# Down-projection of two MLP slices as seven block products: a Strassen-like scheme carried from the up-projection into the down-projection

## The reference

```
def _squared_relu_mlp(h, w1, w2):
    return jnp.square(jax.nn.relu(h @ w1)) @ w2
...
x = x + _squared_relu_mlp(_rmsnorm(x, norm_mlp[i]), mlp_w1[i], mlp_w2[i])
```

## Time and profile before

| what | value |
|---|---|
| median of 3 runs | 2006.91 us |
| the profiled execution | 2007.59 us, span 2005.8 us |
| busy: PE, PEld, DVE, ACT, POOL | 1993.7, 1743.6, 1376.8, 1062.6, 304.9 us |
| granted TensorE clock | 1.000 |
| HBM read | 223.05 MB |

### The profile page before, as it was taken

How to read it: one execution, slowest core, us unless ns; L and a number is a source line. 1 busy time by engine, 2 the same in 40 slices (tenths; PEclk the granted TensorE clock), 3 DMA queues, 4 the chain that set the end, 5 groups by cost and what they waited for, 6 DMA issues and landing times.

```text
span 2005.8 us, 28783 instructions
## 1 busy us (share of the span) xinstructions
PE 1993.7 (99%) x11760; PEld 1743.6 (87%) x11760; DVE 1376.8 (69%) x1634; ACT 1062.6 (53%) x1508; POOL 304.9 (15%) x371
## 2 busy tenths in 40 slices
PE   9999999999999999999999999999999999999998
PEld 7888898989878889899888889898988888899897
DVE  6866865655898777556698786564687758656564
ACT  6655643625467646254456663453547646354363
POOL 7102000000200200002731200000741011000000
PEclk9999999999999999999999999999999999999999
DMA  6212455545222264474332145544532123474651
GB/s 189 68 59 66 142 128 159 146 95 158 89 90 84 86 166 141 102 190 102 117 90 71 54 150 143 156 132 112 163 83 72 55 72 122 110 193 102 160 145 42
DMA packets 190610, 230.94 MB, mean 115 GB/s; under 512 B 18864, under 2 KB 133104, under 8 KB 190480
## 3 DMA queue, kind: packets, MB, share of 16 engines
q1 hardware_dynamic: 158192, 198.62, 31.7%
q0 software_dynamic: 29888, 29.11, 9.2%
q10 hardware_dynamic: 2400, 1.38, 0.2%
HBM read 223.05 MB, written 2.10 MB: 112 GB/s over the span
## 4 chain that ended last, share of the span: by engine, by line
PE 95%; DVE 2%; POOL 1%; ACT 0%; issue 0%; DMA 0%; DVEq 0%; ACTq 0%; POOLq 0%
PE psum L708 29%; PE psum L710 29%; PE psum L709 29%; PE psum L1151 2%; PE psum L1124 1%; PE psum L1259 1%; DVE h_lo L1544 1%; PE psum L1100 1%; PE psum L1096 1%; PE psum L1095 1%; PE psum L1101 1%; PE psum L1094 0%; PE psum L1361 0%; PE psum L1391 0%; PE psum L1377 0%
## 5 line engine op out<-in xcount | busy, mean ns | idle before, releaser
L1517 DVE TENSOR_TENSOR w_lo<-w_raw,w_hi 128x1024 fp32r<-128x1024 f32 (+1 forms) x307 | 378.4, 1237 | 255.7 <-ACT w_hi L2456 254.3
L2456 ACT ACTIVATE w_hi<-w_raw 128x1024 fp32r<-128x1024 f32 (+1 forms) x311 | 328.5, 1061 | 386.1 <-PE psum L710 362.5
L708 PE MATMUL psum<-u_hi,w_hi 128*128 128x512 f32 x1256 | 492.4, 392 | 1.2 <-issue 1.2
L710 PE MATMUL psum<-u_hi,w_lo 128*128 128x512 f32 x1256 | 489.2, 389 | 0.0
L709 PE MATMUL psum<-u_lo,w_hi 128*128 128x512 f32 x1256 | 489.1, 389 | 0.0
L708 PE MATMUL psum<-h_hi,w_hi 128*128 128x256 f32 (+1 forms) x1368 | 440.6, 322 | 1.7 <-DVE w_lo L1517 1.3
L709 PE MATMUL psum<-h_lo,w_hi 128*128 128x256 f32 (+1 forms) x1368 | 437.4, 320 | 0.0
L710 PE MATMUL psum<-h_hi,w_lo 128*128 128x256 f32 (+1 forms) x1368 | 437.3, 320 | 0.0
L708 PEld LDWEIGHTS psum<-u_hi,w_hi 128*128 128x128 f32 x1256 | 235.9, 188 | 50.9 <-issue 1.9
L708 PEld LDWEIGHTS psum<-h_hi,w_hi 128*128 128x128 f32 x1368 | 260.2, 190 | 22.2 <-DVE w_lo L1517 1.8
L710 PEld LDWEIGHTS psum<-u_hi,w_lo 128*128 128x128 f32 x1256 | 235.8, 188 | 49.6
(11 more groups left out here) (342 smaller groups left out, 2662.9 us busy)
## 6 DMA issues: line engine op xcount, KB each, us to landing
w_raw<-in_mlp_w SPq DMA_DIRECT2D x192, 512.0 KB, 3.9
arena<-in_mlp_w SPq DMA_DIRECT2D x88, 512.0 KB, 4.7
w_raw<-in_mlp_w POOLq DMA_DIRECT2D x36, 512.0 KB, 7.2
w_raw<-in_mla_w_o SPq DMA_DIRECT2D x16, 512.0 KB, 3.7
w_raw<-in_lru_w_in SPq DMA_DIRECT2D x16, 512.0 KB, 3.8
arena<-in_mlp_w POOLq DMA_DIRECT2D x12, 512.0 KB, 6.6
w_raw<-in_swa_w_in SPq DMA_DIRECT2D x12, 512.0 KB, 3.9
w_raw<-in_mla_w_ukv SPq DMA_DIRECT2D x8, 512.0 KB, 4.7
```

What stands on the lines that cost most here:

```text
L708: nc.tensor.matmul(out, stat[0], mov[0], start=start, stop=False, skip_group_check=skip)
L710: return nc.tensor.matmul(out, stat[1], mov[0], start=False, stop=stop, skip_group_check=skip)
L1517: ins = nc.vector.tensor_tensor(w_lo[:, to], tile, exact(w_hi[:, to]), ALU.subtract)
L2456: nc.scalar.activation(w_hi[:, to], raw_tile(op.raw), ACT.Copy).then_inc(w_hi_done, 1)
```

## The change

In slices 1 and 2 of every MLP (`TURNED_DOWN`), the eight units of the down-projection become two rounds (g = 0, 1) of seven products, 14 units of 24 matmuls over 256 columns. For this the relu output is first multiplied by the norm factor and then squared (so the down result can be added to x as it is), and four sums of its blocks are formed on VectorE ("turned"), all seven operands being split. Results are added to x straight out of PSUM in nine steps per round, in place of `add_scaled`. Up rounds of these slices are `scaled_round`. Not shown: `group` is moved out of `seven_products` unchanged, cos and sin share a tile, `w2_block` names 512 x 256 blocks of w2, and the raw buffer of the sum p is declared free two products earlier.

```diff
+    def blocks_of(block):
+
+        a, e, b = (Raw(block(half, n), phase, True) for half, n in ((0, 0), (1, HALF), (1, 0)))
+        p = Raw(block(0, 0), phase, True, plus=block(0, HALF))
+        q = Raw(block(0, HALF), phase, True, plus=block(1, HALF))
+        return a, e, b, p, q
+
...
-        q.freed = len(ops)
+        p.freed = q.freed = len(ops)
...
-        p.freed = b.freed = len(ops)
...
+    def seven_down(i, s, g):
+
+        nonlocal sums
+
+        def block(half, n):
+            return ("w2_block", i, s * SLICE + half * T, g * T + n, BLOCK)
+
+        a, e, b, p, q = blocks_of(block)
+        raws.extend((a, q, b, p, e))
+        ops.append(Operand("A11", a))
+        a.freed = len(ops)
+        ops.append(Operand("A21+A22", q))
+        q.freed = len(ops)
+        ops.append(Operand("A12", b))
+        ops.append(Operand("A11+A21", p, (p, e)))
+        ops.append(Operand("A11+A21+A22", p, (b, p), made=sums + 1))
+        ops.append(Operand("A22", e))
+        p.freed = e.freed = len(ops)
+        ops.append(Operand("A11+A12+A21+A22", b, made=sums + 2))
+        b.freed = len(ops)
         sums += 2
 
...
             for g in range(2):
+                if s in TURNED_DOWN:
+                    seven_down(i, s, g)
+                    continue
...
+TURNED_DOWN = (1, 2)
...
+        minus_t1, t1_raw = tile(u_lo_f32, 1), tile(u_lo_f32, 0)
+        U11 = tile(u_hi, 0), tile(arena_r, relu_at), kept[0][0]
+        UT1 = tile(u_hi, 1), tile(u_lo, 0), t1_raw
+        U21 = tile(u_hi, 2), tile(u_lo, 2), kept[1][0]
+        UT3 = tile(u_hi, 3), tile(arena_r, relu_at + 1), kept[0][1]
+        UT2 = tile(u_lo, 3), tile(u_lo, 1), minus_t1
+        UT4 = sq_r[:, :], tile(arena_r, tables_at), kept[1][0]
+        U22 = trig_r[:, :], tile(arena_r, tables_at + 1), kept[1][1]
...
+            def seven_down(g):
+
+                xy, own = (0, 1) if g == 0 else (2, 3)
+                d = c.now("downs")
+                c.add("downs")
+                n = 7 * (d // 2)
+                x1, y, z, v = bank(xy, 0), bank(xy, 1), bank(own, 0), bank(own, 1)
+                claim(xy)
+                pe.wait_ge(u_turned, n + 1)
+                group(x1, U11, False)
+                claim(own)
+                pe.wait_ge(u_turned, n + 2)
+                group(v, UT1, False)
+                pe.wait_ge(u_turned, n + 3)
+                group(y, U21, False)
+                pe.wait_ge(u_turned, n + 4)
+                group(z, UT3, False)
+                pe.wait_ge(u_turned, n + 5)
+                pe.wait_ge(x_added, 7 * d + 1)
+                group(x1, UT2, True)
+                pe.wait_ge(u_turned, n + 6)
+                pe.wait_ge(x_added, 7 * d + 5)
+                group(z, UT4, True)
+                pe.wait_ge(u_turned, n + 7)
+                pe.wait_ge(x_added, 7 * d + 7)
+                group(x1, U22, True)
...
+                    if s in TURNED_DOWN:
+                        seven_down(0)
+                        seven_down(1)
+                    elif last and s + 1 == SLICES:
...
+            def u_low(n, k, operand):
+
+                high, low, raw = operand
+                dve.wait_ge(u_high, 7 * n + k)
+                nc.vector.tensor_tensor(low, raw, exact(high), ALU.subtract).then_inc(u_turned, 1)
+
+            def by_rstd(to, source, j):
+
+                k = to.shape[1] // HALF
+                rows = rstd[:, j * HALF:(j + 1) * HALF].unsqueeze(1).to_broadcast([P, k, HALF])
+                return nc.vector.scalar_tensor_tensor(out=by_chunk(to), in0=by_chunk(source), scalar=0.0, in1=rows,
+                                                      op0=ALU.max, op1=ALU.mult)
+
+            def scaled_round(g, n):
+
+                xy, own = (0, 1) if g == 0 else (2, 3)
+                first, other = kept[g]
+                d11, d21, d12, d22 = first[:, 0:T], first[:, T:2 * T], other[:, 0:T], other[:, T:2 * T]
+                r = c.now("rounds")
+                c.add("rounds")
+                c.add("tensor_unit", 3)
+                split(1)
+                if g == 1:
+                    dve.wait_ge(u_squared, 4 * n + 2)
+                    nc.vector.tensor_tensor(t1_raw, *kept[0], ALU.subtract).then_inc(u_turns, 1)
+                split(1)
+                if g == 1:
+                    u_low(n, 1, U11)
+                split(1)
+                product_passed()
+                dve.wait_ge(c_copied, 3 * r + 1)
+                nc.vector.tensor_tensor(d11, bank(xy, 1), d11, ALU.add).then_inc(c_added, 1)
+                split(1)
+                product_passed()
+                dve.wait_ge(c_copied, 3 * r + 3)
+                nc.vector.tensor_tensor(d22, d22, bank(xy, 0), ALU.subtract).then_inc(c_added, 1)
+                if g == 1:
+                    u_low(n, 2, UT1)
+                split(1)
+                product_passed()
+                free(nc.vector.tensor_tensor(d21, bank(own, 0), d21, ALU.subtract), own)
+                dve.wait_ge(c_added, 2 * r + 2)
+                by_rstd(d22, d22, 1)
+                dve.wait_ge(area_free[own], c.now(f"area{own}"))
+                by_rstd(first, first, 0).then_inc(scaled, 1)
+                split(1)
+                product_passed()
+                free(by_rstd(d12, bank(xy, 0), 1), xy)
+                split(1)
...
+            def seven_down(g, n):
+
+                xy, own = (0, 1) if g == 0 else (2, 3)
+                d = c.now("downs")
+                c.add("downs")
+                x1, y, z, v = (by_chunk(bank(xy, 0)), by_chunk(bank(xy, 1)), by_chunk(bank(own, 0)),
+                               by_chunk(bank(own, 1)))
+                x11, x12, x21, x22 = (x_block(g, i, j) for i in range(2) for j in range(2))
+
+                def add(to, sums, after, op=ALU.add):
+                    dve.wait_ge(x_added, 7 * d + after)
+                    return nc.vector.tensor_tensor(to, to, sums, op)
+
+                if g == 0:
+                    u_low(n, 3, U21)
+                    dve.wait_ge(u_squared, 4 * n + 4)
+                    nc.vector.tensor_tensor(kept[0][1], kept[0][1], kept[1][1], ALU.subtract).then_inc(u_turns, 1)
+                    dve.wait_ge(u_high, 7 * n + 2)
+                    nc.vector.tensor_tensor(minus_t1, minus_t1, kept[1][1], ALU.subtract).then_inc(u_turns, 1)
+                product_passed()
+                add(x11, x1, 0).then_inc(x_added, 1)
+                split(1)
+                if g == 0:
+                    u_low(n, 4, UT3)
+                    dve.wait_ge(u_turns, 4 * n + 3)
+                    nc.vector.tensor_tensor(kept[1][0], kept[1][0], minus_t1, ALU.add).then_inc(u_turns, 1)
+                    u_low(n, 5, UT2)
+                product_passed()
+                add(x22, v, 0, ALU.subtract).then_inc(x_added, 1)
+                add(x12, v, 0).then_inc(x_added, 1)
+                split(1)
+                product_passed()
+                add(x11, y, 1).then_inc(x_added, 1)
+                if g == 0:
+                    u_low(n, 6, UT4)
+                product_passed()
+                add(x22, z, 2).then_inc(x_added, 1)
+                split(1)
+                if g == 0:
+                    u_low(n, 7, U22)
+                split(1)
+                product_passed()
+                add(x21, x1, 0, ALU.subtract).then_inc(x_added, 1)
+                add(x22, x1, 5, ALU.subtract).then_inc(x_added, 1)
+                split(1)
+                product_passed()
+                free(add(x21, z, 6), own)
+                split(1)
+                product_passed()
+                free(add(x12, x1, 3), xy)
+                split(1)
+                for a in (own, xy):
+                    dve.wait_ge(area_free[a], c.now(f"area{a}"))
...
+                    if s in TURNED_DOWN:
+                        n = c.now("downs") // 2
+                        for g in range(2):
+                            scaled_round(g, n)
+                        for g in range(2):
+                            seven_down(g, n)
+                        continue
...
+            def u_high_of(operand):
+
+                high, low, raw = operand
+                nc.scalar.activation(high, raw, ACT.Copy).then_inc(u_high, 1)
+
+            def square_in_place(t):
+                nc.scalar.activation(t, t, ACT.Square).then_inc(u_squared, 1)
+
+            def scaled_round(g, n):
+
+                xy, own = (0, 1) if g == 0 else (2, 3)
+                first, other = kept[g]
+                d11, d21, d12, d22 = first[:, 0:T], first[:, T:2 * T], other[:, 0:T], other[:, T:2 * T]
+                r = c.now("rounds")
+                c.add("rounds")
+                product_passed()
+                if g == 0:
+                    act.wait_ge(u_ready, c.now("u_ready"))
+                nc.scalar.activation(d11, bank(xy, 0), ACT.Copy).then_inc(c_copied, 1)
+                split(1)
+                if g == 1:
+                    u_high_of(U11)
+                split(1)
+                if g == 1:
```

(51 more changed lines are left out.)

55 lines of the change are left out of this document (36 added, 19 removed).

## The result

| | before | after |
|---|---|---|
| median of 4 runs | 2006.89 us (2006.59 to 2007.75) | 2110.53 us (2109.27 to 2112.02) |
| the profiled execution | 2007.59 us, span 2005.8 | 2112.02 us, span 2110.2 |
| HBM read | 223.05 MB | 248.21 MB |

The changed kernel takes 1.0516 times as long (95% interval 1.0498 to 1.0534): 103.6 us more, where 102 were forecast.

The account below looks back on a forecast made before the run. TensorE, busy 99% of the span, was taken as the bound. 28 products of 2.86 us plus six stalls gave 96.3 us a slice against 83.54, 102 us more over 8 slices: 2110 us, range 2062 to 2132.

Parts of the forecast that it names:

- What TensorE gains: Changed slice: 14 products replace 8 units, 40.04 us instead of 43.52, a gain of 3.48 us, 27.8 in all.
- What the helpers get: Changed slice: VectorE's 72.7 us fit TensorE's 80.1, but 24.8 against 20.0 us in g = 0, so order decides.
- The costs without a row before: New scaling steps on VectorE: taken at the times of plain sums; the upper bound used 0.75 us for 512 columns.
- The walk: Hand walk through a changed slice's handovers: TensorE stalls of 1.3, 1.0, 6.0, 5.0, 1.2 and 1.7 us.
- P18: 18th product, down-projection g = 0: TensorE stalls 5.0 us, waiting for VectorE's low part of UT3.
- The clock rival: TensorE's clock falls in the stalls, a product takes at least 5.1 us: 0 to 2 us a slice, 2110 to 2126; chance 0.25.
- The period: Time between like rows of changed slices: near 96 us, 96.3 by the sum, against 83.54 before.
- the tightest load: Sum p of g = 1: load lands about 78, split due at 76.7, product at 85; costs nothing, might cost 1 us.
- "No stall" in g = 1: Second down round: VectorE has 15.7 us of work in 20 us and catches up, so TensorE has no stall.
- "Too dark": Rival: stalls before the 17th and 18th products are half as long, a slice takes 90.8 us, time 2065; chance 0.13.
- "hidden": Rival: a slice's stalls together fall under 3.48 us, TensorE stays the bound; 1980 with none; chance 0.05.

Follow-up runs that it names:

- `e_both_light`: Changed kernel with steps reordered and ScalarE's copies earlier, both sums of weights of g = 0 left out, three sums of squares cut to 8 columns: 2000.26 us.
- experiment 5: Changed kernel with the same steps of ScalarE and VectorE in another order, all work kept, copies not moved: 2039.87 us.
- experiment 7: Changed kernel with one VectorE sum of weights per changed slice left out: 2099.39 us where left out in g = 0, 2107.94 us in g = 1.
- Experiments 6 and 8: Changed kernel, steps reordered and ScalarE's copies earlier: 2030.92 us; also without two sums of weights: 2013.28 us; sums of squares cut too: 2000.26 us.
- experiment 4: Changed kernel with down products multiplying blocks of h instead of the seven operands, without waits for them; helpers' steps all stay: 2112.96 us.
- `e_kept_warm`: Changed kernel with 44 matmuls, their result overwritten, run ahead of the 17th product's wait for U21: 2108.01 us.

## Why the prediction was right, step by step

**What TensorE gains.** The term was 3.48 us a slice. A trace without stalls can't be had, but `e_both_light` bounds it from below: with 1.7 us of stalls its slice takes 82.3 against 83.54, so about 2.9 us were gained before the stalls. The term was right in kind and some 0.5 us too large, since a product comes to 2.88 there, with all that isn't a stall in it. The 109 ns that the Trainium skill gives as the gap of a single matmul of 256 columns by itself (TensorE: Matmul & The Clock Gate, Back-to-back issue gap) don't appear in the changed stretches either; in P18 of the trace after they start 0.12 us apart.

**What the helpers get.** VectorE's total fits, as predicted (75% busy), and the order decides: shown twice, by the order alone (experiment 5, 71 us) and by the one row at two places (experiment 7). The 24.8 us of work against 20.0 us of products in g = 0 were named, but the text let "order decides" stand for the whole. Experiments 6 and 8 show two layers: some 80 us are the order (103.6 to 24.3 with both edits), and of the rest 17.6 us go with two rows of VectorE. That 24.3 us is the least that any order gives isn't shown; by the amounts alone an estimate is 15 us, 8 x (24.8 - 20.0 - 2.9).

**The costs without a row before.** The scaling steps were taken at plain sums' times, 1.22 and 0.68 us, with 0.75 as the bound for 512 columns. After, they last those times (the view of line 1849 of the kernel after: durations in ns as min/median/max, first and last start, forms; the smallest of the first row is of 512 columns, the largest of 1024):

```profile
L1849 DVE SCALAR_TENSOR_TENSOR arena<-arena,rstd x32: 676/946/1217, 291.9 to 1961.2; 128x512 f32<-128x512 f32 x16, 128x1024 f32<-128x1024 f32 x16
L1849 DVE SCALAR_TENSOR_TENSOR arena<-psum,rstd x16: 681/683/684, 296.9 to 1966.8; 128x512 f32<-128x512 f32 x16
```

**The walk.** In the slice shown five of six stalls came within 0.3 us; that P20's did is in part luck, since in six of eight slices a slow P18 takes its place. The low part of U21 was put at 52.8 from the slice's start (its end, 54.05, less 1.22) and started at 52.4 (833.60, with P1 at 781.2). The walk's long list of handovers held because each handover was read from a row of its own and the order is written out by hand.

**P18.** This one was off: 2.64 us for 5.0. The walk let P17 run at full clock. It took 5.20 us, 2.34 more, and the stall behind it shrank by as much; P18 started 7.84 us after P17 and 7.9 were predicted. The sum didn't change.

**The clock rival.** Its mechanism came true and its price didn't. The granted clock fell in the stall before P17 (0.84 and 0.59 by stretch, 1.00 in P18 of the slice shown), as the rival said, and the slow product took 5.20 us where it gave "at least 5.1". It also said that P18's wait would take that up, and this held. In six slices part of P18 was slow as well (in slice 2 of layer 2 the granted clock is 0.68 from 938.70 to 944.00), which the rival didn't have; P20 then starts 0.2 to 0.4 us later and P21 at the same distance from P17. Of the "0 to 2 us" it cost 0. The rule of the Trainium skill that an idle TensorE drops to half its clock and gets it back under sustained work (TensorE: Matmul & The Clock Gate, Part 1) agrees with these rows.

**The period.** Between like sums of slice 1 and slice 2 it is 96.10 and 95.97 us in layers 1 and 2, 96.3 predicted, and 98.31 and 97.15 in layers 3 and 4; with the second slices the mean of all eight is 96.7. (The loads of a slice were put at 146 GB/s; from 781 to 877 us the profile has 149.) The longer ones go with a load: in g = 1 of every changed slice one of ScalarE's splits waits 5.6 to 8.1 us for an accumulating load. The prediction had seen it as the tightest load and put it at nothing. That is right in three slices, as in this one, where ScalarE waits 5.92 us for it and TensorE doesn't:

```profile
859.81 1.06 ACT L2660 ACTIVATE w_hi<-w_raw 128x1024 fp32r<-128x1024 f32 x1 [5.92 <-DMA w_raw<-in_mlp_w]
```

Where ScalarE waits 6.6 to 6.8 us for it (three slices) TensorE has a stall of 0.5 us before P28, and where it waits 7.5 and 8.1 us (slice 1 of layers 4 and 3) stalls of 1.2 and 1.9 us before P27 and P28 together. "No stall" in g = 1 was therefore too bright, by 4.6 us over the eight slices. The rows of these stalls name VectorE's sum into x or no releaser; that the load is behind them is read from this order alone, and no run here takes it away.

**The rivals that fell.** "Too dark" (2065) would have needed stalls half as long; "hidden" (1980) needed all stalls of a slice under 3.48 us. `e_both_light` gets there with 1.7 us of stalls, but only with two of VectorE's rows left out and three cut to 8 columns.

## What to carry to other kernels

Before fewer matmuls are bought with more work on helpers, add up the helper's rows in the stretch where its result is due, not over the whole loop: here 72.7 us fitted into 80.1 and 24.8 didn't fit into 20.0. Then walk through the two helpers' lists by hand: where each waits for the other, one can be idle a quarter of the time and the other half of it, and they bound the kernel all the same, and reordering their steps was worth 71 of 104 us without one instruction less. A wait removed by itself tells little, since the next thing from the same list takes its place (experiment 4); the same step removed at two places tells which one is on the line.

## What had not been expected of the hardware

A TensorE that runs at half rate can cost nothing. 44 added matmuls kept P17 at full rate and only moved the slow product to P18; P18 started 7.84 us after P17 either way. TensorE was slow behind idle times of 5.76 us (P17 in the kernel after) and 4.70 us (P18 in `e_kept_warm`). Behind the slow P17 and 2.64 us of idle time it was in full from the second matmul of P18 in two slices of the kernel after; in the other six it ran 12 to 17 matmuls of P18 at half rate, and P21 started no later for it.
